# The solve levels of a chunked scan on half of the columns, with the next products placed between the transposes

## What is computed

```
def step(state, inp):
    r_t, w_t, k_t, v_t, a_t, b_t = inp
    sa = jnp.einsum('bhvk,bhk->bhv', state, a_t)
    state = (state * w_t[:, :, None, :]
             + sa[..., None] * b_t[:, :, None, :]
             + v_t[..., None] * k_t[:, :, None, :])
    y_t = jnp.einsum('bhvk,bhk->bhv', state, r_t)
    return state, y_t
...
_, y = lax.scan(step, state0, (r, decay, k, v, a, b))
```

## Time and profile before

| | us |
|---|---|
| median of 3 runs | 1447.78 (1446.91 to 1450.87) |
| the profiled execution | 1449.46 |
| its span in the profile | 1447.6 |
| PE busy in the span | 1389.6 |
| DVE busy | 883.7 |
| ACT busy | 718.1 |
| the scan's two rounds | from about 774 to 884 of the span |

### The profile page before, as it was taken

One profiled execution on the slowest core, in us unless ns is written; L12 is line 12 of the kernel. 1 busy time (PEld: TensorE's weight loads), 2 busy tenths in 40 slices (PEclk: granted clock), 3 DMA queues, 4 the chain that ended last, 5 costly groups with the idle time before them and its releaser, 6 DMA issues.

```text
span 1447.6 us, 24101 instructions
## 1 busy us (share of the span) xinstructions
PE 1389.6 (96%) x10302; PEld 1177.3 (81%) x10302; DVE 883.7 (61%) x1231; ACT 718.1 (50%) x995; POOL 144.1 (10%) x143
## 2 busy tenths in 40 slices
PE   8989999999999999999999978999999988899998
PEld 8966988987897998886567866899997765699997
DVE  5655655557577655565977678465556665555563
ACT  5454654445645545445573433454445655444452
POOL 0063011100000001100100112000000133000000
PEclk9999999999999999999999999999999999999999
DMA  8743565566556565555655001465464531266472
GB/s 289 231 122 97 190 205 174 163 201 189 188 147 205 196 199 186 188 156 184 170 166 162 12 10 47 143 219 191 149 229 155 194 102 56 63 217 189 140 231 82
DMA packets 91188, 232.87 MB, mean 161 GB/s; under 512 B 20535, under 2 KB 26311, under 8 KB 90955
## 3 DMA queue, kind: packets, MB, share of 16 engines
q1 hardware_dynamic: 90520, 229.22, 49.7%
q0 software_dynamic: 560, 2.11, 0.4%
HBM read 228.14 MB, written 1.08 MB: 158 GB/s over the span
## 4 chain that ended last, share of the span: by engine, by line
PE 87%; DVE 6%; ACT 3%; POOL 1%; issue 1%; DMA 0%; SPq 0%; DVEq 0%; POOLq 0%; ACTq 0%
PE PS L452 84%; PE PS L455 4%; POOL SM L2254 1%; POOL AB L2375 1%; ACT SH L1152 1%; DVE AB L1671 1%; DVE SL L1567 1%; ACT XH L1152 1%; ACT AB L1149 0%; DVE XL L1561 0%; DVE XX L1561 0%; DVE XN L1561 0%; DMA ST<-in_w_attn_in 0%; DVE X L1567 0%; DVE LG L1561 0%
## 5 line engine op out<-in xcount | busy, mean ns | idle before, releaser
L1567 DVE SCALAR_TENSOR_TENSOR SL<-ST,SM,SH 128x1024 fp32r<-128x1024 f32 (+1 forms) x256 | 314.6, 1249 | 167.6 <-ACT SH L1152 166.2
L1152 ACT ACTIVATE SH<-ST,SM 128x1024 fp32r<-128x1024 f32 (+1 forms) x256 | 282.1, 1121 | 185.7 <-PE PS L452 115.4
L452 PE MATMUL PS<-XH,SH 128*128 128x256 f32 x1224 | 345.0, 282 | 1.9 <-DVE XL L1561 1.9
L452 PE MATMUL PS<-XH,SL 128*128 128x256 f32 x1224 | 345.1, 282 | 0.0
L452 PE MATMUL PS<-XL,SH 128*128 128x256 f32 x1224 | 344.1, 281 | 0.0
L1561 DVE TENSOR_TENSOR SL<-ST,SH 128x1024 fp32r<-128x1024 f32 (+1 forms) x153 | 194.6, 1286 | 147.9 <-ACT SH L1152 147.7
L1152 ACT ACTIVATE SH<-ST 128x1024 fp32r<-128x1024 f32 (+1 forms) x153 | 158.7, 1052 | 159.8 <-PE PS L452 127.0
L452 PEld LDWEIGHTS PS<-XH,SH 128*128 128x128 f32 x1224 | 232.1, 190 | 3.2 <-DVE XL L1561 2.0
L452 PE MATMUL PS<-SH,XH 128*128 128x512 f32 x544 | 223.4, 411 | 11.2 <-DVE XL L1561 8.0
L452 PEld LDWEIGHTS PS<-XL,SH 128*128 128x128 f32 x1224 | 229.8, 188 | 0.9
L452 PEld LDWEIGHTS PS<-XH,SL 128*128 128x128 f32 x1224 | 229.9, 188 | 0.2
(11 more groups left out here) (253 smaller groups left out, 1411.9 us busy)
## 6 DMA issues: line engine op xcount, KB each, us to landing
ST<-in_ffn_w_gu SPq DMA_DIRECT2D x80, 512.0 KB, 4.7
ST<-in_w_mlp_up SPq DMA_DIRECT2D x64, 512.0 KB, 4.7
ST<-in_w_mlp_down SPq DMA_DIRECT2D x64, 512.0 KB, 4.4
ST<-in_ffn_w_down SPq DMA_DIRECT2D x44, 512.0 KB, 4.4
ST<-in_w_attn_in SPq DMA_DIRECT2D x24, 512.0 KB, 4.8
ST<-in_w_conv_in SPq DMA_DIRECT2D x24, 512.0 KB, 4.5
ST<-in_w_ple_gate SPq DMA_DIRECT2D x16, 512.0 KB, 4.3
ST<-in_kv_w SPq DMA_DIRECT2D x16, 512.0 KB, 3.9
```

The lines of the kernel that those rows point to most:

```text
L452: return e.matmul(o, l, r, start=start, stop=stop, skip_group_check=True)
L1152: return e.activation(o, x, ACT.Copy, **kw)
L1567: return e.scalar_tensor_tensor(o, x, a, y, op, op2)
```

## The change

Two things are done at once.

The products and DVE's steps of levels 0 to 3 are narrowed. In a level that joins blocks of j = 2, 4, 8 or 16 columns, only the even blocks' columns change. The products of below read the even blocks' 32 columns of `XX` (in runs of j) and not all 64; those of grow read 32 columns of `Z`; `Z` has 128 elements a partition and not 256; and the sum into `XX` adds 128 elements and not 256, but as two instructions of 64 elements (the strided form has one dimension too many for one instruction). The masks in the constants are packed to match. Level 4 is as it was, apart from its mask's place.

PE's order within a level is changed: the products of below of a lane stand after the flip of the next lane, and not after all flips.

```
@@ tensor_program @@
+def even(x, n):
+    return x.rearrange("p (b two j) -> p b two j", two=2, j=2 << n)[:, :, 0, :]
...
     def lane_below(p, z, n):
         w.wait_ge(*at("xt", p, n))
         for m, c, h in QUADS:
-            t = mm(ob(z, c, m * 64, 64, h), z.LG[half(c), h, m, 0:64], z.XX[half(c), m, h, :], True, True)
+            if n < 4:
+                o = ob(z, c, m * 32, 32, h).rearrange("p (b j) -> p b j", j=2 << n)
+                t = mm(o, z.LG[half(c), h, m, 0:64], even(z.XX[half(c), m, h, :], n), True, True)
+            else:
+                t = mm(ob(z, c, m * 64, 64, h), z.LG[half(c), h, m, 0:64], z.XX[half(c), m, h, :], True, True)
...
     def lane_grow(p, z, n):
         w.wait_ge(*at("z", p, n))
         if n < 4:
             for m, c, h in QUADS:
-                t = mm(ob(z, h, m * 64, 64, c), z.XT[half(h), m, c, :], z.Z[half(h), c, m, :], True, True)
+                t = mm(ob(z, h, m * 32, 32, c), z.XT[half(h), m, c, :], z.Z[half(h), c, m, 0:32], True, True)
...
         for n in range(5):
-            for p, z in lanes:
-                lane_flip(p, z, n)
-            for p, z in lanes:
-                lane_below(p, z, n)
+            for t in range(5):
+                if t < 4:
+                    lane_flip(*lanes[t], n)
+                if 1 <= t < 5:
+                    lane_below(*lanes[t - 1], n)
             for p, z in lanes:
                 lane_grow(p, z, n)
@@ vector_program @@
     def lane_below(p, z, n):
         w.wait_ge(*at("below", p, n))
-        tt(z.Z[:, :, :, :], z.two[:, :, 0:128].rearrange("p c (m j) -> p c m j", m=2), m4(C_LV + 64 * n, 64), ALU.mult).then_inc(*inc("z", p, n))
+        k, c = (32, 32 * n) if n < 4 else (64, 256)
+        tt(z.Z[:, :, :, 0:k], z.two[:, :, 0:2 * k].rearrange("p c (m j) -> p c m j", m=2), m4(C_LV + c, k), ALU.mult).then_inc(*inc("z", p, n))
 
     def lane_grow(p, z, n):
-        xp = z.XX[:, :, :, :].rearrange("p m b j -> p b m j")
         w.wait_ge(*at("grown", p, n))
-        tt(xp, xp, z.two[:, :, 0:128].rearrange("p b (m j) -> p b m j", m=2), ALU.add).then_inc(*inc("xx", p, n + 1))
+        for b in range(2):
+            x = z.XX[:, :, b, :].rearrange("p m (k two j) -> p m k two j", two=2, j=2 << n)[:, :, :, 0, :]
+            t = tt(x, x, z.two[:, b, 0:64].rearrange("p (m k j) -> p m k j", m=2, j=2 << n), ALU.add)
+        t.then_inc(*inc("xx", p, n + 1))
```

More of the change, by code:

```diff
@@ L48, in constant_array @@
         m = 2 << n
-        c[:, C_LV + 64 * n:C_LV + 64 * (n + 1)] = ((r6 // m) % 2 == 1) & ((q6 // m) == (r6 // m) - 1)
+        level = ((r6 // m) % 2 == 1) & ((q6 // m) == (r6 // m) - 1)
+        if n < 4:
+            c[:, C_LV + 32 * n:C_LV + 32 * (n + 1)] = level.reshape(128, 32 // m, 2, m)[:, :, 0].reshape(128, 32)
+        else:
+            c[:, C_LV + 256:C_LV + 320] = level
     c[:, C_SUI:C_SUI + 128] = same & (r < q)
```

## The result

The changed kernel takes 1468.0 us (median of 17 runs, 1453.5 to 1473.1), the kernel before 1449.3 beside it (17 runs, 1446.9 to 1453.0): a ratio of 1.010, 95% interval 1.0083 to 1.0116 (worked out from all runs; the two medians alone stand at 1.013). It is slower, and by more than the range of the prediction allows. Its profiled execution took 1468.48 us with a span of 1466.7, 19.1 more than before.

The account below looks back on a forecast made before the run. PE, busy 96% of the span, was taken to bound the kernel; round 1's +2.9 us and round 2's +1.6 made +4.5, so 1454.0 profiled and 1452.3 for the median, with 8 in 10 within 1446 to 1460.

Parts of the forecast that it names:

- The walk: PE's steps through one level, timed from its first flip: grow at 3.27, 4.3 us per level against 3.69.
- the likeliest case: The walk as told, with its own range of 1449.5 to 1455.5 us; chance 0.60.
- DVE's part: DVE's `Z` and `XX` steps: operations 0.20 and 0.135 us apart, saving 0.8 us per level if short runs cost nothing.
- PE's part, width: PE's products at 32 columns: 0.059 us per group as at 64, a gain of nothing; bounds 0 and half.
- PE's part, order: Eight tiling changes per level for two, 0.09 us each, and below 0 waiting for ACT's copy until 0.91: level 4.3 us.
- The sum: All levels added up: round 1 +2.9 us, round 2 +1.6, together +4.5.
- the stall of 0.59: PE's stall for instructions in round 1's levels 1 to 3: kept in the sum, may fall under a wait (-0.6).
- The falling clock: Rival: PE's waits for copies bring half clock, a level some 6.45 us, four of seven levels, 1461 us; chance 0.14.
- Free changes of tiling: Rival: tiling changes on PE cost nothing by themselves; level 3.65 us, total +0.5, 1448.3 us; chance 0.14.
- DVE's pace: Rival: DVE sets the pace throughout, 2.7 us per level, -6, 1441.8 us; chance 0.12, shared with half-price products plus hidden stall.

Follow-up runs that it names:

- experiment 4: Changed kernel with each product of levels 0 to 3 doubled to 64 columns, second copy read by nobody; DVE narrow, changed order: 1452.6 us, ratio 1.0023.
- experiment 9: Experiment 4 with products of 32 columns in levels 1 to 3 of round 1 alone: 1452.3 us, ratio 1.0010.
- experiment 11: Experiment 4 with products of 32 columns in levels 1 to 3 of both rounds, level 0 still doubled: 1459.1 us, ratio 1.0066.
- experiment 1: The kernel before with only PE's order changed, all widths as they were: 1453.3 us, ratio 1.0030.
- experiment 2: The changed kernel with the old order of PE, so that only the widths change: 1453.7 us, ratio 1.0030.
- experiment 5: The changed kernel with four extra products of 128 columns, read by nobody, in each of levels 0 to 3: 1474.4 us, ratio 1.0176.
- experiment 8: The kernel before with extra products of 128 columns in round 2 before the last lane's below, 3 at level 0, 18 at level 1: 1449.5 us, ratio 1.0012.
- experiment 3: The changed kernel with the old order of PE and products of levels 0 to 3 doubled to 64 columns, DVE narrow: 1447.2 us, ratio 0.9987.

## Why the prediction was wrong

The forecast was 1452.3, within 1446 to 1460. The walk behind it holds; the likeliest case was the wrong one. Point by point:

- **DVE's part** is right: 0.193 and 0.131 us for 0.20 and 0.135; short runs of elements cost nothing (eight half `XX` take 1.14 us at level 0, in runs of 2, and at level 3, in runs of 16, in experiment 4); and in round 1's levels 1 to 3 DVE waits for PE before every `Z`.
- **PE's part, width** is right in what it says and wrong in what it leaves out. Four lanes of grow take 1.11 us at 64 columns (experiment 4), and a level at 32 columns (experiment 9) 4.22 for 4.30. From "a gain of nothing on PE" I went on as if 32 columns changed nothing on PE. They do: with them a clock that is down stays down longer. **This is the step that failed.** The changed kernel was at half clock for 34 us in round 1 and 38 in round 2; experiment 4, which differs in the columns alone, for none and 14: +18.7 us against +4.5. The two statements of the Trainium skill that the prediction sets against each other don't part here: "TensorE: Matmul & The Clock Gate", section "Back-to-back issue gap", has one and the same spacing for all products of 1 to 64 columns, so by it too nothing is saved between 64 and 32. That agrees with the rows, though the spacing itself is another (0.059 us per group).
- **PE's part, order** is right: 0.91, 1.30, 1.67, 3.25 and 4.30 in experiment 4 for 0.91, 1.30, 1.66, 3.27 and 4.3.
- **The sum** is right in size (experiment 4: +4.5, interval +1.2 to +5.5) and less so in its terms. Round 1 gives +1.6 (20.52 from first flip to last grow, for 18.96) where I had +2.9. Level 0 lasts 4.37, not 5.1: only the first two flips wait for `MG` and stand 0.6 apart, the other two start at 1.36 and 2.13, where I had 1.9 and 2.85; and the 4.80 of before held half clock (0.57 in 784 to 788), which I hadn't looked at. Levels 1 to 3 last 12.90 for 13.5, since the stall of 0.59 is gone under the waits, as the prediction allowed. Level 4 is right (3.25 for 3.27). Round 2 gives +1.4 for +1.6, and that is luck: levels 0 and 1, in part at half clock, take 14.50 us for 14.06 before, where I had 0.8 less, and level 2, at full clock, 4.52 for 5.37, where I had 0.5 more; levels 3 and 4 are right (+0.9 and +1.0). Where the clock stays up until 846 (experiment 11) levels 0 and 1 take 13.27, the 0.8 less that I had. The other 1.5 of the 4.5 is not in the levels and I can't place it: the profiled run of experiment 4 took 1449.3 us, 3.3 below its median.
- **The falling clock**, given 0.14, is what happened. Its price of a level was right (6.38 for 6.45), its reason and its reach were not. I tied it to how long PE waits within a level; experiments 1 and 4 have these waits and are at full clock throughout round 1, experiment 2 has none of them and is at half clock for 20 us. I let it hold four levels of seven; it held nearly everything from round 1's level 1 up to the products of 128 columns, in both rounds, some 70 us in all: 1468 for 1461.
- **Free changes of tiling** and **DVE's pace** fall: no level of 3.65 or 2.7 us in this order.

The row that would have helped was in the trace of before and I read past it: 0.57 in 784 to 788 with PE busy 3.91 of 4 us, and 1.00 right behind. The clock can fall at the entry to the levels in any of these kernels (in round 1 it fell in seven of the thirteen profiles, in round 2 in all but those of experiments 5 and 8), and each then relies on something to bring it back. I asked what could make it fall and not what makes it rise. The Trainium skill invites the same slip: "TensorE: Matmul & The Clock Gate", section "What's actually happening", says that the gate goes by how busy PE has been and that activity releases the throttle. Read with the profile's busy time, this case doesn't agree: PE is busy 21.86 of 22.00 us and the clock stays at 0.50; the rows decide.

## What to carry to other kernels

Making products narrower is not free even where they don't get shorter and PE looks full: before doing it, look in the trace for short stretches at half clock near them, since the wide products may be what ends these. When a clock rival is weighed, ask two things apart, what brings it down and what brings it back, and price the second by the distance to the next wide products: in all five stretches here that outlasted the levels the clock rose 1.5 to 3.2 us after the first products of 128 columns behind them had begun. And products placed between steps that wait for another engine cost the delay of the last step, not only the switch.

## What the runs showed of the hardware

- At full clock products of 32 columns in the 64 by 64 tiling can leave the clock where it is (13.4 us at 1.00 in experiment 9; 32 us at 1.00, with extra products between, in round 2 of experiment 5).
- At half clock they can hold it there with PE busy nearly all the time: 34 and 38 us in the changed kernel, 27 in round 2 of experiment 11. In the same order with 64 columns the clock came back after 14 us (experiment 4), in the kernel before after at most 7. In the old order it came back among products of 32 columns too, after 20 us in round 1 of experiment 2. Why narrow products differ I can't say from these runs.
- Extra products of 128 by 128 between them didn't bring the clock back in round 1 of experiment 5; in its round 2 the clock never fell.
- PE's stalls put down to `issue` grow as the levels get shorter: 0.59 us in levels 1 to 3 where a level takes 3.69, 2.07 where it takes 3.07 (experiment 3), none where it takes 4.3 (experiment 4).
- A product of 128 columns on the whole array, which is two records, takes 0.24 us at full clock.
